# Chunk pieces, low parts and block signals of a two-block fp32 network on one Trainium2 core

## The reference

```python
def ada_modulation(c, w, b):
    mod = jax.nn.silu(c) @ w + b
    shift, scale, gate = jnp.split(mod, 3, axis=-1)

def recurrent_block(h, w_in, conv_w, conv_b, w_a, b_a, w_x, b_x, lam, w_out):
    z = h @ w_in
    xr, gate = jnp.split(z, 2, axis=-1)
    xr = centred_depthwise_conv(xr, conv_w, conv_b)
    y = rg_lru(xr, ..., reverse=False) + rg_lru(xr, ..., reverse=True)
    return (y * jax.nn.gelu(gate)) @ w_out

def sq_relu_mlp(h, w1, w2):
    return jnp.square(jax.nn.relu(h @ w1)) @ w2

def first_block(...):
    for i in range(DEPTH):                       # 2 layers
        h = x * (1.0 + scale) + shift
        y = windowed_gqa(h, ...) if i == 0 else recurrent_block(h, ...)
        x = layer_norm(DN_ALPHA * x + (1.0 + gate) * y, ln_g[i, 0], ln_b[i, 0])
        y = sq_relu_mlp(x * (1.0 + scale) + shift, mlp_w1[i], mlp_w2[i])
        x = layer_norm(DN_ALPHA * x + (1.0 + gate) * y, ln_g[i, 1], ln_b[i, 1])
    return x
```

## Time and profile before

| what | value |
|---|---|
| median of three runs | 1420.08 us |
| the profiled execution's own time, its span | 1423.08 us, 1421.8 us |
| mean granted clock of TensorE, share of full | 0.955 |
| PE busy | 1303.8 us (92%) |
| DVE busy | 1024.0 us (72%) |
| ACT busy | 703.1 us (49%) |
| HBM read | 305.82 MB, mean 216 GB/s |
| chain that ended last, by engine | PE 78%, DVE 12%, DMA 5%, ACT 3% |

### The profile page before, as it was taken

One profiled execution on the slowest core, in us unless ns is written; L12 is line 12 of the kernel. 1 busy time (PEld: TensorE's weight loads), 2 busy tenths in 40 slices (PEclk: granted clock), 3 DMA queues, 4 the chain that ended last, 5 costly groups with the idle time before them and its releaser, 6 DMA issues.

```text
span 1421.8 us, 19701 instructions
## 1 busy us (share of the span) xinstructions
PE 1303.8 (92%) x7700; PEld 1161.1 (82%) x7700; DVE 1024.0 (72%) x1462; ACT 703.1 (49%) x968; POOL 0.4 (0%) x5
## 2 busy tenths in 40 slices
PE   6978799999998994999995999998899999999986
PEld 6767699999877884999994788997788878878775
DVE  5666687777677896777776748866567769678685
ACT  3432455553357843454452643433457657566563
POOL 0000000000000000000000000000000000000000
PEclk9969999999999997999998999999799999999998
DMA  8728787776386764766651542220158869788772
GB/s 335 264 69 314 270 307 275 277 276 257 112 317 237 264 226 177 292 232 223 248 178 64 183 134 77 90 88 12 69 198 279 317 236 334 269 288 302 237 254 88
DMA packets 82685, 308.16 MB, mean 217 GB/s; under 512 B 9313, under 2 KB 9569, under 8 KB 81825
## 3 DMA queue, kind: packets, MB, share of 16 engines
q1 hardware_dynamic: 80352, 292.59, 58.1%
q10 hardware_dynamic: 2240, 14.31, 2.6%
HBM read 305.82 MB, written 1.05 MB: 216 GB/s over the span
## 4 chain that ended last, share of the span: by engine, by line
PE 78%; DVE 12%; DMA 5%; ACT 3%; issue 2%; SPq 0%; DVEq 0%; ACTq 0%
PE ps L465 77%; DMA ring<-stream 4%; DVE junk L424 2%; DVE w_low L424 2%; DVE ti L424 1%; ACT w_high L424 1%; DVE rs L424 1%; DVE hsc L424 1%; PE ps L1105 1%; DVE y_experts L424 1%; DVE y L424 0%; DVE sc L424 0%; DVE t_one L424 0%; DVE x L424 0%; DVE sm L424 0%
## 5 line engine op out<-in xcount | busy, mean ns | idle before, releaser
L424 DVE TENSOR_TENSOR w_low<-ring,w_high 128x1024 fp32r<-128x1024 f32 x368 | 442.4, 1222 | 164.6 <-ACT w_high L424 161.7
L424 ACT ACTIVATE w_high<-ring 128x1024 fp32r<-128x1024 f32 x368 | 385.7, 1058 | 314.8 <-PE ps L465 205.8
L465 PE MATMUL ps<-x_high,w_high 128*128 128x256 f32 (+1 forms) x784 | 234.6, 299 | 27.2 <-DVE x_low L424 21.1
L465 PE MATMUL ps<-x_high,w_low 128*128 128x256 f32 (+1 forms) x784 | 232.6, 297 | 0.0
L465 PE MATMUL ps<-x_low,w_high 128*128 128x256 f32 (+1 forms) x784 | 232.1, 296 | 0.0
L424 DVE CUSTOM_DVE_ANT_0 junk<-ring,cond 128x1024 f32<-128x1024 f32 x137 | 166.9, 1223 | 39.6 <-DMA ring<-stream 30.5
L465 PEld LDWEIGHTS ps<-x_high,w_high 128*128 128x128 f32 x784 | 152.2, 194 | 36.5 <-issue 12.3
L465 PEld LDWEIGHTS ps<-x_low,w_high 128*128 128x128 f32 x784 | 151.9, 194 | 2.7
L465 PEld LDWEIGHTS ps<-x_high,w_low 128*128 128x128 f32 x784 | 151.1, 193 | 3.2
L465 PE MATMUL ps<-h_high,w_high 128*128 128x256 f32 x512 | 144.5, 282 | 1.7 <-DVE h_low L424 1.0
L465 PE MATMUL ps<-h_high,w_low 128*128 128x256 f32 x512 | 144.6, 282 | 0.0
(11 more groups left out here) (318 smaller groups left out, 1953.2 us busy)
## 6 DMA issues: line engine op xcount, KB each, us to landing
ring<-stream SPq DMA_DIRECT2D x364, 512.0 KB, 4.9
ring<-moe SPq DMA_DIRECT2D x192, 512.0 KB, 4.9
gw<-gw ACTq DMA_DIRECT2D x1, 3840.0 KB, 14.0
tab_two<-tab ACTq DMA_DIRECT2D x1, 2824.0 KB, 14.9
cond<-cvec ACTq DMA_DIRECT2D x2, 512.0 KB, 5.4
x<-xT ACTq DMA_DIRECT2D x1, 1024.0 KB, 11.7
ctx_first<-ctxT ACTq DMA_DIRECT2D x1, 1024.0 KB, 5.0
ctx<-ctxT ACTq DMA_DIRECT2D x1, 1024.0 KB, 4.8
```

The lines of the kernel that those rows point to most:

```text
L424: return op(*a, **k).then_inc(self.sem, 1)
L465: return pe.matmul(out, stationary, moving, start=start, stop=stop, skip_group_check=True)
```

## The change

1. Places of the chunks. Chunks 14 to 17 of the second block leave the recurrent stage and become second chunks of MLP1's turns 0 to 3. The stage's 16 chunks in the `z` part are spread otherwise (one at tiles 4, 6, 8 and 10, two at the others, where before the first six had two and the last four one), and its `o` part keeps four chunks of eight, at the first four pieces.
2. VectorE's order at the stage's end: two chunks, the third group, two chunks, the constants, the last group, the sums into x.
3. Low parts. The last low parts ahead of a norm move behind the sums into x, to between the norm's constants and its reciprocal: three at the first norm (before: two ahead of the sums, two there; the fourth now comes in the MLP), four at the third (before: ahead of the sums), one at the fourth (before: in MLP1's last turn). The constants ahead of the fourth norm's sums move ahead of MLP1's last turn.
4. The table load for the first norm's root moves ahead of three high parts on ScalarE.
5. Signals. The scaled, high and low parts of x are counted by block instead of by pair, TensorE waits block by block (`first_tiles`, `first_z`, the second block's first tiles, the router), and VectorE alternates scaled and low parts.

```diff
-A2_TURNS = ((0,), (1,), (2,), (3,), (4,), (5,), (), ())
-A2_ORDER = [8, 9, 10, 11, 12, 13, 14, 6, 15, 16, 7, 17] + list(range(6)) + list(range(18, 24))
-RNN_CHUNKS = {("z", t): 2 if t < 8 else 1 for t in range(2, NT)} | {("o", t): 1 for t in (0, 1, 2, 3, 5, 6, 9, 10)}
+A2_TURNS = ((0, 14), (1, 15), (2, 16), (3, 17), (4,), (5,), (), ())
+A2_ORDER = [8, 9, 10, 11, 12, 6, 13, 7, 0, 14, 1, 15, 2, 16, 3, 17, 4, 5] + list(range(18, 24))
+RNN_CHUNKS = {("z", t): 1 if t in (4, 6, 8, 10) else 2 for t in range(2, NT)} | {("o", t): 1 for t in range(4)}
...
     def first_tiles(w0, x_low):
-        for p in range(4):
-            pe.wait_ge(s.x_low, x_low + p)
+        for k in range(KT):
+            pe.wait_ge(s.x_low, x_low + k)
...
     def layer_norm(r):
-        A(m.MISC[:, 14:15], m.par("eps5"), ACT.Sqrt)
+        if r > 0:
+            A(m.MISC[:, 14:15], m.par("eps5"), ACT.Sqrt)
...
-    high_upto(W_MLP0 + 4)
+    A(m.MISC[:, 14:15], m.par("eps5"), ACT.Sqrt)
+    high_upto(W_MLP0 + 3)
...
         scaled(0)
-        for p in range(4):
-            if p < 3:
-                scaled(p + 1)
+        for k in range(KT):
+            if k < KT - 1:
+                scaled(k + 1)
             if n != MOD_LN1:
-                lower(p)
+                lower(k)
...
-        if r == 0:
-            low_upto(W_MLP0 + 4)
+        low_upto({0: W_MLP0 + 3, 1: W_RNN, 2: W_MLP1 + 4, 3: W_IN2 + 4}[r])
         root(n_root)
...
-        if n2 == 3:
-            low_upto(W_MLP0 + 2)
...
-            low_upto(w + 12)
+            low_upto(w + (12 if t < 15 else 11))
...
-    chunks(("o", 0), ("o", 1), ("o", 2), ("o", 3))
+    chunks(("o", 0), ("o", 1))
     group(2)
-    chunks(("o", 5), ("o", 6))
-    last_group()
-    chunks(("o", 9), ("o", 10))
-    low_upto(W_MLP1 + 4)
+    chunks(("o", 2), ("o", 3))
     bias(72, 24, "ada_b", 72)
     op(vv.tensor_scalar, m.gate1, m.MOD[:, 64:72], 1.0, None, ALU.add)
+    last_group()
     vv.wait_ge(s.x_next, 16)
     evacuate(1, W_MLP1, m.gate1)
```

More of the change, by code:

```diff
@@ L154, in x_splits @@
 def x_splits(n):
-    return 4 * (n - (n > MOD_LN1))
+    return KT * (n - (n > MOD_LN1))
 def split_upto(w):
@@ L411, in __init__, with __call__ @@
         self.engine, self.own, self.sem, self.counts = engine, own, None, {}
-    def __call__(self, op, *a, inc=None, apart=False, **k):
+    def __call__(self, op, *a, inc=None, by=1, apart=False, **k):
         if apart == "two":
@@ L422, in __call__ @@
         self.sem = inc or self.own
[L423 to L424 removed]
+        self.counts[self.sem] = self.counts.get(self.sem, 0) + by
+        return op(*a, **k).then_inc(self.sem, by)
 def load_program(nc, m, s, arrived, stream, moe, outT):
@@ L594, in tensor_program @@
             ada_piece(E_PIECES[2], PS[:, 6, 2:3])
-    pe.wait_ge(s.t2, 4)
+    pe.wait_ge(s.t2, KT)
     pe.wait_ge(s.ones, 1)
@@ L652, in first_tiles @@
     def first_tiles(w0, x_low):
-        for p in range(4):
-            pe.wait_ge(s.x_low, x_low + p)
+        for k in range(KT):
+            pe.wait_ge(s.x_low, x_low + k)
             for n in range(3):
-                if p == 0:
+                if k == 0:
                     pe.wait_ge(s.w_low, split_upto(w0 + n + 1))
-                for k in (2 * p, 2 * p + 1):
-                    ins = mm3(PS[:, n // 2, (n % 2) * 256:(n % 2 + 1) * 256], weight(w0 + n, k * P), pair(XIN, slice(None), k), k == 0 and n != 1, k == KT - 1)
-                if p == 3:
+                ins = mm3(PS[:, n // 2, (n % 2) * 256:(n % 2 + 1) * 256], weight(w0 + n, k * P), pair(XIN, slice(None), k), k == 0 and n != 1, k == KT - 1)
+                if k == KT - 1:
                     ins.then_inc(s.used, 1)
@@ L1165, in scalar_program, with A @@
     split = [0]
-    def A(out, in_, func, inc=None, **k):
-        op(act.activation, out, in_, func, inc=inc, **k)
+    def A(out, in_, func, inc=None, by=1, **k):
+        op(act.activation, out, in_, func, inc=inc, by=by, **k)
     def high_upto(w):
@@ L1191, in modulated @@
         for p in range(4):
-            act.wait_ge(s.t2, 4 * n + p + 1)
-            A(m.XH[:, s_, 2 * p:2 * p + 2, :], m.T2[:, 2 * p:2 * p + 2, :], ACT.Copy, s.x_high, apart=True)
+            act.wait_ge(s.t2, KT * n + 2 * p + 2)
+            A(m.XH[:, s_, 2 * p:2 * p + 2, :], m.T2[:, 2 * p:2 * p + 2, :], ACT.Copy, s.x_high, 2, apart=True)
     def first_x(p):
@@ L1556, in scalar_program @@
     for k in range(KT):
-        if k % 2 == 0:
-            act.wait_ge(s.t2, 4 * MOD_MOE + k // 2 + 1)
-        A(m.T2[:, k, :], m.T1[:, k, :], ACT.Identity, s.x_high if k % 2 else None, bias=m.MOD[:, 120 + k:121 + k], apart=True)
+        act.wait_ge(s.t2, KT * MOD_MOE + k + 1)
+        A(m.T2[:, k, :], m.T1[:, k, :], ACT.Identity, s.x_high, bias=m.MOD[:, 120 + k:121 + k], apart=True)
     act.wait_ge(s.in_att, 32)
@@ L2250, in vector_program @@
     for k in range(KT):
-        op(vv.scalar_tensor_tensor, m.T1[:, k, :], m.X[:, k, :], sc2[:, k:k + 1], m.RSTD, ALU.mult, ALU.mult, inc=s.t2 if k % 2 else None, apart=k > 0)
+        op(vv.scalar_tensor_tensor, m.T1[:, k, :], m.X[:, k, :], sc2[:, k:k + 1], m.RSTD, ALU.mult, ALU.mult, inc=s.t2, apart=k > 0)
     ROUT = m.ROUT
```

55 lines of the change are left out of this document (23 added, 32 removed).

## The result

The changed kernel takes 1408.24 us (median of four runs, 1404.77 to 1411.73), the kernel before 1420.27 in the same comparison (1417.21 to 1422.93). The ratio is 0.9913, 95% interval 0.9896 to 0.9930: faster by 0.9%, 12 us. The profiled execution took 1411.73 us with a span of 1410.4, against 1421.8 before, so the two traces differ by 11.4 us, and these are what is accounted for here.

A forecast was written before the change was run, and what follows sets the result against it. TensorE's own records bound the MLP turns; elsewhere it waits at the norms and in the recurrent stage. Terms 3.5 + 0.85 + 17.0 - 1.35 - 3.9 + 6.5 + 0.4 = 23.0 off 1420.08 gave 1397.1 us, range 1388 to 1406.

The forecast's parts named there:

- Recurrent stage, its products: TensorE's products in the recurrent stage, claimed to end at 531 instead of 534.55.
- Tile 6: Recurrent stage: the ring-piece stall of 2.64 us and its cold stretch go, 4.3 us gained.
- the out product's first piece: Recurrent stage: the piece comes late, a new stall of 2.4 us and a cold stretch of 1.7.
- Tile 9: Recurrent stage: half of the 4.42 us ring-piece stall goes, 2.2 us; its cold stretch stays.
- Both old stalls stay and the new one comes: Late bound for the end of the recurrent stage's products: 536.
- no new stall and the second one gone: Early bound for the end of the recurrent stage's products: 528.4.
- Rival B: Recurrent stage: products do not end earlier (ring's stalls stay, end at 536) or `y` comes last; 1404 us, chance 0.18.
- The stage's end: Recurrent stage: sums run beside the last tile, mean right behind it, `t_one` 3.7 us later; 13.5 us gained.
- MLP1's three waits: Starts of MLP1's turns 1 to 3: stalls on a low part of 1.9, 1.2 and 0.8 us, 3.9 lost.
- C: Norms and MLP1: the added waits do not show, low parts hidden, no stall in MLP1; 1389 us, chance 0.14.
- D: No change: chunks in MLP1 hold up the ring, eight turns lose 2.5 us each; 1418 us, chance 0.04.
- E: Slower: TensorE stays cold from the out product's first piece over 12 tiles; 1445 us, chance 0.04.

The follow-up runs named there:

- all together with pairs: Changed kernel with dots of tiles 7 and 10 ahead of groups, low parts ahead of sums, second chunks in MLP1's turns 2 to 5, pair signals: 1396.35 us, 0.9831.

## Why the prediction was wrong, and where it was right

**The step that failed: "Recurrent stage, its products".** It let the products end 3.5 us earlier; they end 3.1 us later against the stage's start, 6.6 of the 11.6 us missing. Tile 6 was right (3.6 us gained, forecast 4.3), and behind the out product's first piece some 1.5 us came back, where the prediction had some 1.2 for small waits. Of the other two:

- Tile 9. The prediction let half of the wait go, 2.2 us, because one chunk fewer lies in the queue. The wait shrank by 0.6 and the cold stretch grew by 1.3. The length of the queue was not what held the piece: with the dots of tile 7 ahead of VectorE's first group the wait falls to 0.50, and with the old spread it stays at 3.81.
- The out product's first piece. The mechanism was named in the prediction, and its size was wrong: 2.4 of wait and 1.7 of cold run were booked, 5.5 and 2.0 came. The issue came about where it was reckoned, 3 us behind the group. A stall of 2.4 puts the landing at 483.0, that is 4.9 us behind an issue at 478.1; the prediction gave "3.4 us or more" for it, from the earlier trace rows, and it took 7.6. It had four pieces queued ahead of this one in its own text, and yet booked a time of rows in which fewer were in flight. In the six kernels that keep this part of the changed kernel the wait is 5.37, 4.06, 3.91, 4.09, 3.50 and 3.67 us: always there, above the 2.4 booked, and the changed kernel's own profiled execution, the slowest of its four runs, shows the largest.

The bounds of this step do not follow from its own terms either. "Both old stalls stay and the new one comes" is 534.55 + 4.1 = 538.7 and not 536, and "no new stall and the second one gone" is 534.55 - 4.3 - 6.1 = 524.1 and not 528.4. In before's time, with TensorE's lead of 2.7 us taken off, the products ended at 537.6: outside the stated bounds, inside those of the terms. Rival B with 538.7 comes to 1407 and not to 1404, above the range's upper end of 1406.

So the first half of rival B (the ring's waits stay, the products end at 536) was right; its second half, a late `y`, did not come. Its 1404 was nearest to the 1408 measured, and 0.18 was too little for it. Its argument "the ring's order only moves stalls" had rows to rest on. In before's chain of the work that ended last, the piece of tile 9 already leaves behind dots that stand behind a group:

```profile
441.14 0.96 DVE y L424
442.10 1.14 DVE junk L424
...
444.62 1.14 DVE junk L424
445.80 5.29 DMA ring<-stream
451.23 38.36 PE ps L465 x168
```

The counter-argument, fewer chunk pieces in the stage, says nothing on when a slot is released.

**Not in the forecast.** Signals by block move the end of the first tile later, 0.7 us at each of the two MLPs; the prediction weighed only the start of the product, and the run with the last two blocks by tile shows the cause, and that only the one in MLP1 can be won back. The longer cold stretch behind the first norm cost 1.2, and the second block lost 1.3 in small steps although the router's norm gained 0.8; no experiment settles these two.

**What was right.** The stage's end: sums directly behind the last `y`, mean without a wait, `t_one` 3.65 us behind it, 13.7 us for 13.5. The first norm (3.5 for 3.5: low parts bind) and the third (-1.5 for -1.35), confirmed by taking the low parts away from there, which gives 5.67 us again. The four low parts ahead of the third reciprocal took 4.62 us (at 542.22), 1.15 apiece, so the 0.3 us more that the prediction worked out from a page's rule did not come. The Trainium skill, "VectorE: DVE Perf Modes", section "The DRAIN you can't avoid", itself adds to that rule that an operation which is not held starts earlier. MLP1's three waits (4.1 for 3.9), which are gone when the chunks stand in later turns. The second norm (0.8 for 0.85) and the fourth (4.8 for 5.3, and 1.1 for the 1.2 of the blocks). Rivals C, D and E did not come: C's hidden waits showed in full, and no tile behind the out product's first stayed cold for long.

**What stays open.** Signals by block give 0.8 to 1.2 us at each norm's next product in two pairs of traces, but neither pair of totals shows it: in one the recurrent stage ran 5.5 us shorter with pairs, in the other the medians differ by less than their spread. How the 6.6 us missing in the recurrent stage divide between the kernel and the one execution that was profiled stays open too, since kernels with the same stage gain up to 4.6 us on that trace there. Why behind waits of one length the clock is sometimes low and sometimes not wasn't settled either.

## What to carry to other kernels

In a ring that one queue fills in order, look for what holds a late piece in the work that stands ahead of the *release* of the slots before it, on whatever engine releases them. The number of pieces in the queue was the right thing to count at tile 6, ahead of the first group, but not at the two places behind a group: follow each late piece to its releasing instruction, look what long block of work stands ahead of that, and move the release in front of it. Take the landing time of a piece from rows where as many others were in flight. When a signal is made finer at the start of a product, look also at when the product's first tile ends, because the next stage hangs on that.

## What the runs showed of the hardware

In these traces a ring piece of 512 KB lands 3.4 us after its issue at the quickest, but 6.7 and 7.6 us with others in flight.

Whether a wait costs a cold run as well is not told by its length. At tile 9 the wait was 3.77 us with the chunks in later turns, and the next sixteen records took 5.38; it was 3.75 with pair signals and 3.66 with MLP1's second dots behind, and they took 3.69. The busy time by stretch behind the last of these waits:

```profile
441.00:444.40 3.40, 3.36 (x16) 3.00 (x17) 3.18 (x7) 2.88 (x6) 0.00 (x0) 1.00 1.01 408
```

The granted clock is 1.00, 2.4 GHz. With the low parts ahead of the sums, a shorter wait of 3.30 us was followed by a stretch at 0.56:

```profile
438.80:445.40 6.60, 6.58 (x17) 5.36 (x18) 5.50 (x11) 3.22 (x7) 0.00 (x0) 0.56 0.89 362
```

The Trainium skill, "TensorE: Matmul & The Clock Gate", section "HAM oscillation — how this bites in real kernels", says that a wait for DMA that is too long sends the next tile back to the lower clock; these runs agree that it happens, and show waits of nearly one length on either side. So one wait of this size costs between nothing and some 3 us more than itself, and executions of the same kernel differ by up to 9.4 us (1392.56 to 1402.00 us, all together with pairs); edits of 1 to 2 us can be seen in the traces, place by place, but not in the medians here.
